# Latent attention of a two-layer diffusion block on Trainium2: probabilities turned unscaled, the reciprocal row sums applied to each pair of outputs

## What is computed

```python
def attend(q, k, v, ok, sink, scale):
    s = jnp.einsum('bqhgd,bkhd->bhgqk', q, k).astype(jnp.float32) * scale
    ...
        p = jax.nn.softmax(s, axis=-1)
    o = jnp.einsum('bhgqk,bkhd->bqhgd', p.astype(v.dtype), v)
    return o.reshape(o.shape[:2] + (-1,))

def mla_mixer(...):
    qx = mla_q(xm, w_dq, g_q, w_uq, rope)
    kx, vx = mla_kv(xm, w_dkv, g_kv, w_uk, w_uv, rope)
    kh, vh = mla_kv(hm, w_dkv, g_kv, w_uk, w_uv, None)
    ...
    o = lax.map(block, jnp.arange(nb))
    ox = jnp.moveaxis(o, 0, 1).reshape(B, S, -1) @ w_o
```

## Time and profile before

| what | value |
|---|---|
| median of 3 runs | 1676.43 us (1675.84 to 1678.16) |
| the profiled execution's own time | 1678.32 us |
| span of the profiled execution, first to last instruction | 1676.4 us |
| mean granted TensorE clock, share of full | 0.992 |
| TensorE matmul busy | 1646.9 us (98%), 8875 instructions |
| VectorE busy | 1127.7 us (67%) |
| ScalarE busy | 602.8 us (36%) |
| chain of work that ended last | PE 90%, DVE 4%, POOL 2%, ACT 1% |

### The profile page before, as it was taken

How to read it: one execution, slowest core, us unless ns; L and a number is a source line. 1 busy time by engine, 2 the same in 40 slices (tenths; PEclk the granted TensorE clock), 3 DMA queues, 4 the chain that set the end, 5 groups by cost and what they waited for, 6 DMA issues and landing times.

```text
span 1676.4 us, 23648 instructions
## 1 busy us (share of the span) xinstructions
PE 1646.9 (98%) x8875; PEld 1412.2 (84%) x8875; DVE 1127.7 (67%) x1872; ACT 602.8 (36%) x817; POOL 126.2 (8%) x81
## 2 busy tenths in 40 slices
PE   8999999999999899999999999999999999999998
PEld 6788888889877698888888898888888898999997
DVE  5878777777585678777787873463333587666665
ACT  3321222223776542212212332222222356443443
POOL 0000000000796200000000000000000012000000
PEclk7999999999999999999999999999999999999999
DMA  8754554542211035555555423332222222145552
GB/s 303 282 201 181 190 199 188 203 150 99 101 52 51 26 124 194 197 188 203 197 190 187 150 77 125 139 142 95 100 100 100 101 101 76 51 180 194 191 200 76
DMA packets 45427, 247.45 MB, mean 148 GB/s; under 512 B 5169, under 2 KB 5297, under 8 KB 25009
## 3 DMA queue, kind: packets, MB, share of 16 engines
q1 hardware_dynamic: 45360, 246.55, 40.3%
HBM read 245.48 MB, written 1.05 MB: 147 GB/s over the span
## 4 chain that ended last, share of the span: by engine, by line
PE 90%; DVE 4%; POOL 2%; issue 2%; ACT 1%; DMA 0%; SPq 0%; ACTq 0%; POOLq 0%; DVEq 0%
PE ps L1833 13%; PE ps L1835 13%; PE ps L1842 13%; PE ps L1664 10%; PE ps L1665 10%; PE ps L1666 10%; PE ps L2308 5%; PE ps L1691 4%; PE ps L2314 2%; POOL spare L573 2%; PE ps L1950 1%; PE ps L1871 1%; PE ps L2031 1%; PE ps L1905 1%; DVE w_lo L1226 1%
## 5 line engine op out<-in xcount | busy, mean ns | idle before, releaser
L1833 PE MATMUL ps<-a_hi,w_hi 128*128 128x512 f32 x960 | 373.8, 389 | 0.8 <-ACT w_hi L689 0.8
L1835 PE MATMUL ps<-a_lo,w_hi 128*128 128x512 f32 x960 | 373.5, 389 | 0.0
L1226 DVE TENSOR_TENSOR w_lo<-raw,w_hi 128x2048 fp32r<-128x2048 f32 x114 | 260.4, 2287 | 49.4 <-ACT w_hi L689 21.7
L1664 PE MATMUL ps<-h_hi,w_lo 128*128 128x512 f32 (+1 forms) x648 | 234.8, 362 | 1.5 <-POOL h_lo L579 1.4
L1666 PE MATMUL ps<-h_hi,w_hi 128*128 128x512 f32 (+1 forms) x648 | 233.4, 360 | 0.0
L1665 PE MATMUL ps<-h_lo,w_hi 128*128 128x512 f32 (+1 forms) x648 | 233.4, 360 | 0.0
L1842 PE MATMUL ps<-a_hi,w_lo 128*128 128x512 f32 x960 | 227.3, 389 | 0.0
L1833 PEld LDWEIGHTS ps<-a_hi,w_hi 128*128 128x128 f32 x960 | 180.2, 188 | 38.9 <-issue 0.8
L1842 PEld LDWEIGHTS ps<-a_hi,w_lo 128*128 128x128 f32 x960 | 180.2, 188 | 37.4
L1835 PEld LDWEIGHTS ps<-a_lo,w_hi 128*128 128x128 f32 x960 | 180.2, 188 | 37.3
L683 ACT ACTIVATE work<-ps 128x512 f32<-128x512 f32 x66 | 39.4, 598 | 431.5 <-PE ps L1842 419.0
(11 more groups left out here) (352 smaller groups left out, 2517.4 us busy)
## 6 DMA issues: line engine op xcount, KB each, us to landing
raw<-wstream SPq DMA_DIRECT2D x147, 1024.0 KB, 5.0
mring<-wmod SPq DMA_DIRECT2D x144, 512.0 KB, 3.5
spare<-wstream SPq DMA_DIRECT2D x11, 1024.0 KB, 4.8
xT<-tokens SPq DMA_DIRECT2D x4, 512.0 KB, 5.7
cb<-cond SPq DMA_DIRECT2D x1, 1024.0 KB, 7.2
out<-mring SPq DMA_DIRECT2D x4, 256.0 KB, 2.1
mring<-gain SPq DMA_DIRECT2D x1, 512.0 KB, 6.4
cst<-consts SPq DMA_DIRECT2D x1, 449.0 KB, 7.2
```

The source lines that it names most:

```text
L1226: dve.tensor_tensor(w_lo[:, slot], raw[:, slot], w_hi[:, slot].bitcast(F32), ALU.subtract).then_inc(lo_ready, 1)
L1664: pe.matmul(dst, lhs_lo, rhs_hi, start=start, stop=False, skip_group_check=True)
L1833: pe.matmul(bank, hi, a_hi[:, k, 0:nt], start=k == 0, stop=False, skip_group_check=True)
L1835: pe.matmul(bank, hi, a_lo[:, k, 0:nt], start=False, stop=False, skip_group_check=True)
```

## The change

The turn of a unit becomes a plain transpose with the identity as the moving operand, and it no longer waits for the reciprocals. VectorE takes the reciprocals of two units in one instruction at even steps, and `rdiag` goes. At step 2p+4 TensorE spreads the pair's reciprocals along the free axis of all partitions: two products of a broadcast column of `rinv` with the identity, into the free half of the output's PSUM bank. ScalarE copies that to `pair_root` in the same step, behind the high part of the pair before. The value passes wait for this copy (`spread_copy`). VectorE multiplies the pair's output by `pair_root` at the head of step 2p+6 and writes `pair_out`, and the high and low parts are taken from `pair_out` instead of from PSUM.

```diff
@@ -137,7 +137,8 @@
         with ExitStack() as taps:
             tap_buf = sb("tap_buf", [P, TOK], where=taps)
         kr_odd_hi = sb("kr_odd_hi", [P, TOK], F32R)
-        rdiag = sb("rdiag", [P, 2, P])
+        pair_root = sb("pair_root", [P, LAT])
+        pair_out = sb("pair_out", [P, LAT])
         ones = sb("ones", [P, P])
         cst = sb("cst", [P, N_CONST])
         ident_r = sb("ident_r", [P, P], F32R)
@@ -730,10 +730,14 @@
                             act.wait_ge(pv_done, u0 // 2 + e // 2 - 1)
                         act.activation(pt_unit(pt_hi_buf, e, units[e][1]), pt_bank(e, units[e][1]),
                                        ACT.Copy).then_inc(pt_hi, 1)
-                    if i >= 6 and i % 2 == 0:
-                        p = (i - 6) // 2
-                        act.wait_ge(pv_done, u0 // 2 + p + 1)
-                        act.activation(out_to(a_hi, p), ps[O_BANK[p % 2]][:, 0:LAT], ACT.Copy).then_inc(ot_hi, 1)
+                    if i >= 4 and i % 2 == 0:
+                        p = (i - 4) // 2
+                        if p >= 1:
+                            act.wait_ge(o_scaled, u0 // 2 + p)
+                            act.activation(out_to(a_hi, p - 1), pair_out[:], ACT.Copy).then_inc(ot_hi, 1)
+                        if p < len(units) // 2:
+                            act.wait_ge(spread_done, u0 // 2 + p + 1)
+                            act.activation(pair_root[:], ps[O_BANK[p % 2]][:, LAT:TOK], ACT.Copy).then_inc(spread_copy, 1)
                     if i in (5, 8):
                         n = i // 3 - 1
                         act.wait_ge(gate_spread, n + 1)
@@ -1359,6 +1363,14 @@
 
             def attention(units, u0, pt_hi_buf, pt_lo_buf, out_to):
                 for i in range(len(units) + 6):
+                    if i >= 6 and i % 2 == 0 and (i - 6) // 2 < len(units) // 2:
+                        p = (i - 6) // 2
+                        dve.wait_ge(spread_copy, u0 // 2 + p + 1)
+                        dve.wait_ge(pv_done, u0 // 2 + p + 1)
+                        if p >= 1:
+                            dve.wait_ge(ot_lo, u0 // 2 + p)
+                        dve.tensor_tensor(pair_out[:], ps[O_BANK[p % 2]][:, 0:LAT], pair_root[:],
+                                          ALU.mult).then_inc(o_scaled, 1)
                     if i < len(units):
                         h, qts, at = units[i]
                         b = slice(at, at + 1)
@@ -1366,15 +1378,10 @@
                         link(dve.tensor_reduce(smax[:, b], ps[S_BANK[i % 3]][:], AX.X, ALU.max))
                         dve.tensor_scalar(nmax[:, b], smax[:, b], q_scale[:, 1, qts[0][0]:qts[0][0] + 1], None,
                                           ALU.mult).then_inc(nmax_ready, 1)
-                    if 1 <= i < len(units) + 1:
-                        e = i - 1
-                        at = units[e][2]
-                        b = slice(at, at + 1)
-                        dve.wait_ge(exp_done, u0 + e + 1)
-                        link(dve.reciprocal(rinv[:, b], den[:, b]))
-                        if e >= 2:
-                            dve.wait_ge(pt_done, u0 + e - 1)
-                        dve.tensor_scalar(rdiag[:, e % 2], ident, rinv[:, b], None, ALU.mult).then_inc(rdiag_ready, 1)
+                    if i >= 2 and i % 2 == 0 and i <= len(units):
+                        b = slice(units[i - 2][2], units[i - 1][2] + 1)
+                        dve.wait_ge(exp_done, u0 + i)
+                        dve.reciprocal(rinv[:, b], den[:, b]).then_inc(rinv_ready, 1)
                     if i == 1:
                         for n in (6, 7):
                             piece_low("v", n)
@@ -1396,7 +1403,7 @@
                     if i >= 7 and i % 2:
                         p = (i - 7) // 2
                         dve.wait_ge(ot_hi, u0 // 2 + p + 1)
-                        dve.tensor_tensor(out_to(a_lo, p), ps[O_BANK[p % 2]][:, 0:LAT], out_to(a_hi, p).bitcast(F32),
+                        dve.tensor_tensor(out_to(a_lo, p), pair_out[:], out_to(a_hi, p).bitcast(F32),
                                           ALU.subtract).then_inc(ot_lo, 1)
 
             dve.memset(rt[:], 0.0).then_inc(out_free[0], 2)
@@ -1884,27 +1891,36 @@
                             last = pe.matmul(ps[2][:, k * P:(k + 1) * P], gate[:, 5, 0, m:m + 1].to_broadcast([P, P]), ident,
                                              start=True, stop=True)
                         last.then_inc(gate_spread, 1)
+                    if i >= 4 and i % 2 == 0 and i - 4 < len(units):
+                        p = (i - 4) // 2
+                        pe.wait_ge(rinv_ready, u0 // 2 + p + 1)
+                        if p >= 2:
+                            pe.wait_ge(o_scaled, u0 // 2 + p - 1)
+                        for u in range(2):
+                            at = units[2 * p + u][2]
+                            last = pe.matmul(ps[O_BANK[p % 2]][:, LAT + u * P:LAT + (u + 1) * P],
+                                             rinv[:, at:at + 1].to_broadcast([P, P]), ident, start=True, stop=True,
+                                             skip_group_check=True)
+                        last.then_inc(spread_done, 1)
                     if i >= 5 and i % 2:
                         p = (i - 5) // 2
                         h = units[2 * p][0]
                         pe.wait_ge(pt_lo, u0 + 2 * p + 2)
-                        if p >= 2:
-                            pe.wait_ge(ot_lo, u0 // 2 + p - 1)
+                        pe.wait_ge(spread_copy, u0 // 2 + p + 1)
                         for k in range(TOK // P):
                             at = [x[p % 2].rearrange("p a n -> p (a n)")[:, 2 * k * P:2 * (k + 1) * P] for x in pt_buf]
                             last = passes(ps[O_BANK[p % 2]][:, 0:LAT], *v(h, k), *at, k == 0, k == TOK // P - 1)
                         last.then_inc(pv_done, 1)
                     if 2 <= i < len(units) + 2:
                         e = i - 2
-                        pe.wait_ge(rdiag_ready, e + 1)
+                        pe.wait_ge(exp_done, u0 + e + 1)
                         if e >= 2:
                             pe.wait_ge(pt_lo, u0 + e - 1)
                         else:
                             pe.wait_ge(piece_lo, mla_evicted("v", 4 + e))
                         for k in range(TOK // P):
-                            last = pe.matmul(ps[PT_BANK[e % 2]][:, k * P:(k + 1) * P],
-                                             probs[:, e % 3, k * P:(k + 1) * P], rdiag[:, e % 2],
-                                             start=True, stop=True)
+                            last = pe.transpose(ps[PT_BANK[e % 2]][:, k * P:(k + 1) * P],
+                                                probs[:, e % 3, k * P:(k + 1) * P], ident)
                         last.then_inc(pt_done, 1)
                     for k in {len(units): (0,), len(units) + 2: (1, 2)}.get(i, ()):
                         early_out(k)
```

More of the change, by code:

```diff
@@ L288, in build @@
         pv_done = sem("pv_done")
-        rdiag_ready = sem("rdiag_ready")
         v_copy = sem("v_copy")
```

## The result

| | before | changed |
|---|---|---|
| median | 1676.12 us, 20 runs | 1679.12 us, 20 runs |
| ratio to before | | 1.0017, 95% interval 1.001 to 1.0023 |
| span of the profiled execution | 1676.4 us | 1678.3 us |
| start of unit 0's scores in it | 1399.69 us | 1399.60 us |
| from there to the end of the span | 276.7 us | 278.7 us |

The ratio is 2.8 us, between 1.7 and 3.9; the forecast was +1.6. So the change is small, but it is slower by more than the noise.

What follows compares the result with a forecast made beforehand. TensorE, busy 58.01 of 59.00 us in the attention, was taken as the bound. +1.65 us for pairs 3 to 5 and +0.04 in the tail, about +1.6, on 1676.43 gave 1678.0 us; range 1675.0 to 1680.6.

Steps and rivals of the forecast that it cites:

- first three pairs: Attention pairs 0 to 2: value passes start no later than in the kernel before, +0 us.
- pairs 3 to 5: Steady part of the attention: period 6.33 against 5.78 us, +0.55 for each pair, +1.65 us in all.
- The tail: From the end of pair 5's value passes to the end of pair 7's: 8.05 against 8.01 us, +0.04.
- The queue in ScalarE's even step: Exponential, turn's high part, output's high part, then copy at +2.75 us; value passes wait for it, TensorE about 1.2.
- The hand-over from the copy to the value passes: Value passes in the even step start 0.06 us after ScalarE's copy ends, at +3.19.
- Turn 0.36: TensorE's turn of each unit: four passes take 0.36 instead of 0.81 us, 7.2 us gained in 16 units.
- Spread: TensorE's two float32 products per pair take 0.41 us, 3.3 for eight; anything beyond 0.41 is hidden by the wait.
- The scaling on VectorE: Scaling ahead of the even step's maximum: 0.42 us, over 1 us early, so it costs nothing.
- the last output's later low part: Behind the attention's last value passes: 0.5 us later, hidden in the projection with over 1 us left.
- the work counts: Rival for the attention: TensorE's saved work sets the time, pair period 5.16 us, end 4.3 earlier at 1672.1; chance 0.07.
- The clock rival: Attention: TensorE's waits drop its clock to 1.2 GHz, +2.5 us a pair, 20 for eight, about 1698; chance 0.04.

Runs made afterwards that it cites:

- e1: The changed kernel with ScalarE's copy of the spread moved ahead of the exponential in the even step; ratio 0.9972 to the kernel before.
- e2: The changed kernel with ScalarE's copy of the spread third instead of fourth, swapped with the output's high part; ratio 0.9999 to the kernel before.
- e4: The changed kernel with one more ScalarE copy, into an unread tile, ahead of the copy of the spread; ratio 1.0028 to the kernel before.
- e5: The changed kernel with the spreads of pairs 3 to 7 in PSUM bank 2, value passes there not waiting for the copy; ratio 0.9988 to before.
- e3: The changed kernel with its plain transposes written as ordinary products with the identity; ratio 1.0028 to the kernel before.
- e7: e1 with its plain transposes written as ordinary products with the identity; ratio 1.001 to the kernel before.
- e6: The kernel before with plain transposes alone: no reciprocals, diagonals, spread or scaling, outputs left unnormalised; ratio 0.9961 to the kernel before.
- e8: e1 with ScalarE's weight split of step 3 in two halves, behind the exponentials of steps 3 and 4; ratio 0.9967 to the kernel before.

## Why the prediction was right

The forecast was no change beyond 0.2%, with +1.6 us, and the range 1675.0 to 1680.6; 1679.12 is inside. The timed change, 1.7 to 3.9 us by its interval, is a little more than the 1.6. The profiles show +2.0, and the steps below account for it to a tenth: 0.2 in the first three pairs, 1.8 in pairs 3 to 5, 0.1 in the tail (the prediction's own 1.65 and 0.04 are 1.7, not 1.6). The 0.8 us between the profiles and the middle of the timed interval no trace explains; 2.0 itself lies within the interval.

- The queue in ScalarE's even step, the step that carried the forecast, stood as written. Counted from the spread's start at 1429.89, exponential +1.17 (forecast 1.18), high part of the turn +1.94 (1.95), of the output +2.42 (2.42), copy +2.73 (2.75). e1, e2, e4 and e5 show that it causes the time, not only goes with it.
- The hand-over from the copy to the value passes was mis-sized: 0.14 (1433.00 to 1433.14) and not the 0.06 read from VectorE's low part. So the value passes start at +3.25 and not +3.19, and the period is 6.37 and not 6.33. The kernel before had the nearer row: in the first mixer's attention value passes wait for such a copy, and start 0.14 behind its end.

```profile
477.32 0.26 ACT L837 ACTIVATE rspread<-ps 128x128 f32<-128x128 f32 x1
477.72 0.36 PE L1664 MATMUL ps<-ab_pt_hi,h_lo 128*128 128x256 f32 x1 [0.37 <-ACT rspread L837]
```

- Turn 0.36: exact, and e3 and e7 price the product at 0.45 more. The Trainium skill ("Perfetto Trace Analysis", section Transposes) says that a logical transpose should use the transpose and not a matmul; it gives no price, and these traces agree with its direction. Spread 0.44 and not 0.41, hidden by the wait, as written.
- The first three pairs were put at +0: measured from unit 0's scores, the value passes of pair 2 came 0.18 later (1426.78 - 1399.60 against 1426.69 - 1399.69). Pairs 3 to 5 added 1.8 (1.65 forecast).
- The tail was put at 8.05 and took 8.11, 0.1 more than in the earlier trace rows. The value passes of pair 6 started 2.83 after the turn began, where 2.64 stood, and those of pair 7 sooner than written. The profile names VectorE's low part for the wait of pair 6, but the one that this pair needs had ended at 1449.34. The copy ended at 1450.08, 0.14 before the value passes, so it was the copy that they waited for.
- The scaling on VectorE cost nothing, and neither did the last output's later low part: TensorE has no wait for either.
- The rival "the work counts" (4.3 us saved) was right as a sum of TensorE's work and wrong as a forecast of this kernel: e1 gains 4.7, close to it, once the queue is out of the way. What the prediction said for this rival was misread: ScalarE busy 33.23 of 59.00 us is idle for 44% of the stage, not for more than half.
- The clock rival did not come: the granted clock stayed at 1.00 in the attention although TensorE's busy time fell to 54.19 of 61.00 us, and to 10.64 of 12.73 in the two periods from 1429.89 (84%; the prediction expected 80). So what the Trainium skill states ("TensorE: Matmul & The Clock Gate", section PE-mode transpose), that transposes do not count as busy like other passes, had no effect to be seen here. The evidence against the rival was thinner than it looked, though. The earlier trace rows are 5 us of a stage in which the clock of the kernel before did fall, twice, the second time after a stretch with TensorE busy for only 1.16 of 4 us:

```profile
528.00:532.00 4.00, 1.16 (x10) 0.78 (x9) 3.31 (x9) 0.68 (x2) 4.00 (x2) 1.00 0.00 0
532.00:536.00 4.00, 4.00 (x17) 3.52 (x17) 0.73 (x3) 3.93 (x11) 1.61 (x3) 0.57 0.71 242
```

## What to carry to other kernels

A change that saves 3.9 us of the bounding engine's work made the kernel 2.0 us slower, and 4.7 us faster after one instruction had been moved. Before timing an edit, write down, for each new wait, the queue of the engine that ends it, in order and from the event that holds its head; the place behind a late exponential was worse than the gap ahead of it. And ask of each wait whether it is for data or for a PSUM bank: a bank wait goes away if another bank is free.

## What the runs showed of the hardware

Two things were not expected.

**The hand-over to TensorE has two sizes.** ScalarE's copy is followed by the value passes that wait for it 0.14 to 0.15 us after its end, in every such row of the changed kernel; VectorE's low part by those of the kernel before after 0.06. It is not a matter of the engine: in the first mixer's attention of the kernel before a turn starts 0.15 behind VectorE's low part.

```profile
559.64 0.69 DVE L1494 TENSOR_TENSOR ab_pt_lo<-ps,ab_pt_hi 128x512 fp32r<-128x512 f32 x1
560.48 0.63 PE L2121 MATMUL ps<-cst,work 128*128 128x128 f32 x4 [1.13 <-DVE ab_pt_lo L1494]
```

In both places with 0.14 or 0.15 the code has two waits ahead of the pass, and the second is the one that ends last; in the place with 0.06 it is the first. Whether that decides it was not tested.

**Identical code ahead of the attention takes up to 4.5 us more or less.** Unit 0's scores start at 1396.41 in e1, at 1399.60 in the changed kernel and at 1400.88 in e2. Of the 4.5 us between e1 and e2, 3.0 go with falls of the granted clock in the first mixer's attention, to the lower level, 1.2 GHz, for three to four us each. From a transpose near 453 us to that stage's last copy of a spread near 565, the executions without a fall (e1, e7) took 110.5 us, those with one (changed, e3, e5, e6) 112.1, and those with two (before, e2, e4, e8) 113.6. So a fall goes with 1.6 us more. One of them, from 500 to 508 us (clock is the number behind the five busy times), in the changed kernel and, without it, in e1:

```profile
500.00:504.00 4.00, 2.25 (x15) 1.86 (x14) 2.52 (x5) 3.20 (x6) 2.09 (x3) 1.00 0.02 6
504.00:508.00 4.00, 4.00 (x14) 3.19 (x13) 3.76 (x10) 2.59 (x6) 2.48 (x3) 0.57 0.00 0
```

```profile
500.00:504.00 4.00, 2.96 (x15) 2.49 (x16) 3.10 (x7) 2.73 (x7) 3.27 (x3) 1.00 0.01 2
504.00:508.00 4.00, 4.00 (x23) 3.02 (x22) 3.89 (x10) 1.60 (x4) 3.40 (x4) 1.00 0.00 0
```

The rest, 1.4 us between e1 and e2 and 1.7 between e1 and the changed kernel, is there before 453 us. The clock is at the lower level for different parts of the first 40 us; from 24 to 32 us, e1, then the changed kernel:

```profile
24.00:32.00 8.00, 7.91 (x54) 4.53 (x53) 7.40 (x11) 3.62 (x5) 0.00 (x0) 0.85 0.59 206
```

```profile
24.00:32.00 8.00, 8.00 (x40) 4.87 (x42) 6.26 (x12) 3.62 (x5) 0.00 (x0) 0.64 0.56 212
```

The changed kernel has the lower mean clock from 0 to 40 us (0.74, e1 0.79), but e2 has that of e1 (0.79) and is 1.4 us behind it all the same. So the mean clock of this stretch is not all of it, and the cause stays open. No edit of this document touches that code, so the falls there say nothing about the change, and for a change of 2 us they are a reason to count from a fixed instruction behind them.
